# Stick-breaking attention: a PSUM column as the scan's unused operand, and each head's next scores behind its scan

## The reference

```python
z = jnp.einsum('bhqd,bhkd->bhqk', qb, kh).astype(jnp.float32) * (dh ** -0.5)
causal = key_pos[None, :] < q_pos[:, None]
log_keep = jnp.where(causal, -jax.nn.softplus(z), 0.0)
log_after = lax.cumsum(log_keep, axis=3, reverse=True) - log_keep
w = jnp.where(causal, jnp.exp(jax.nn.log_sigmoid(z) + log_after), 0.0)
return jnp.einsum('bhqk,bhkd->bhqd', w.astype(vh.dtype), vh)
```

## Time and profile before

| | us |
|---|---|
| median of 3 runs | 3276.93 (3275.43 to 3278.52) |
| profiled execution | 3275.18 |
| its span in the trace | 3273.3 |
| branch 1 of the stage (first scan to last multiply) | 2241.5 to 2418.2, 176.7 |
| PE / DVE / ACT / POOL busy over the span | 95% / 72% / 39% / 25% |

### The profile page before, as it was taken

The page is one execution under the profiler, slowest core; times in us unless marked ns, Lnnn a source line. Parts: engine busy times, 40 slices in busy tenths (PEclk is TensorE's granted clock), DMA queues, the critical chain, the costliest instruction groups (busy, mean ns, idle before and its releaser), DMA issues.

```text
span 3273.3 us, 37086 instructions
## 1 busy us (share of the span) xinstructions
PE 3122.2 (95%) x14322; PEld 2430.9 (74%) x14322; DVE 2345.3 (72%) x3056; ACT 1285.7 (39%) x2044; POOL 832.0 (25%) x810
## 2 busy tenths in 40 slices
PE   7999998998999999999999999998889989999999
PEld 3577785667787788888877888765467877888787
DVE  6655456886546987778888666587744599989896
ACT  5431114552123433334454333376531344444443
POOL 1212100222111243321001344313643114433101
PEclk9999999999999999999999999999899999999999
DMA  6433461006645222227333345531113422222723
GB/s 229 157 137 118 146 211 52 23 23 227 220 163 174 91 90 84 84 85 282 105 126 117 104 129 180 177 116 41 38 60 117 161 81 87 83 84 75 295 88 109
DMA packets 118296, 406.82 MB, mean 124 GB/s; under 512 B 13704, under 2 KB 16328, under 8 KB 113642
## 3 DMA queue, kind: packets, MB, share of 16 engines
q1 hardware_dynamic: 65626, 200.42, 18.9%
q0 software_dynamic: 52496, 204.04, 17.5%
HBM read 321.50 MB, written 82.90 MB: 124 GB/s over the span
## 4 chain that ended last, share of the span: by engine, by line
PE 64%; DVE 8%; ACT 2%; issue 2%; POOL 1%; DMA 0%; ACTq 0%; DVEq 0%; POOLq 0%
PE PS L455 19%; PE PS L456 19%; PE PS L457 19%; PE PS L3316 2%; PE PS L3355 2%; PE PS L3338 1%; DVE HL L411 1%; POOL Sc L3564 1%; DVE E L3490 1%; ACT HL L393 0%; PE PS L2978 0%; DVE HT L1963 0%; DVE H L3616 0%; DVE HTf L1846 0%; DVE cvr L2182 0%
## 5 line engine op out<-in xcount | busy, mean ns | idle before, releaser
L455 PE MATMUL PS<-H,HL 128*128 128x512 f32 x1920 | 759.9, 396 | 15.9 <-DVE H L3616 7.3
L457 PE MATMUL PS<-H,HL 128*128 128x512 f32 x1920 | 751.3, 391 | 0.0
L456 PE MATMUL PS<-H,HL 128*128 128x512 f32 x1920 | 751.3, 391 | 0.0
L393 ACT ACTIVATE HL<-RAW 128x512 fp32r<-128x512 f32 (+1 forms) x429 | 312.0, 728 | 616.5 <-PE PS L457 560.5
L411 DVE TENSOR_TENSOR HL<-RAW,HL 128x512 fp32r<-128x512 f32 (+1 forms) x429 | 402.3, 938 | 141.7 <-ACT HL L393 132.2
L455 PEld LDWEIGHTS PS<-H,HL 128*128 128x128 f32 x1920 | 362.8, 189 | 105.9 <-issue 19.9
L456 PEld LDWEIGHTS PS<-H,HL 128*128 128x128 f32 x1920 | 362.8, 189 | 76.4 <-issue 2.6
L457 PEld LDWEIGHTS PS<-H,HL 128*128 128x128 f32 x1920 | 362.6, 189 | 76.4
L455 PE MATMUL PS<-HT,HL 128*128 128x512 f32 x720 | 282.7, 393 | 17.9 <-DVE rows L2285 15.8
L456 PE MATMUL PS<-HT,HL 128*128 128x512 f32 x720 | 281.7, 391 | 0.0
L457 PE MATMUL PS<-HT,HL 128*128 128x512 f32 x720 | 281.4, 391 | 0.0
(11 more groups left out here) (457 smaller groups left out, 5700.6 us busy)
## 6 DMA issues: line engine op xcount, KB each, us to landing
RAW<-in_w_up SPq DMA_DIRECT2D x100, 512.0 KB, 3.5
RAW<-in_w_down SPq DMA_DIRECT2D x82, 512.0 KB, 3.8
RAW<-in_w_proj SPq DMA_DIRECT2D x48, 512.0 KB, 3.6
scr_hid<-hidr POOLq DMA_DIRECT2D x36, 512.0 KB, 2.9
RAW<-in_w_wmodr SPq DMA_DIRECT2D x32, 512.0 KB, 4.3
HL<-in_w_dfwd POOLq DMA_DIRECT2D x16, 1024.0 KB, 6.8
HL<-in_w_dinv POOLq DMA_DIRECT2D x16, 1024.0 KB, 5.2
RAW<-in_w_wout SPq DMA_DIRECT2D x26, 512.0 KB, 4.5
```

What stands on the lines that cost most here:

```text
L393: e.activation(part_slot(k, p)[0], src, ACT.Copy).then_inc(*k.high.mark(j, x))
L455: e.matmul(out, lh, rh, start=first, stop=False, skip_group_check=goes_on)
L456: e.matmul(out, lh, rl, start=False, stop=False, skip_group_check=goes_on)
L457: return e.matmul(out, ll, rh, start=False, stop=last, skip_group_check=goes_on)
```

## The change

Three things are changed, all in branch 1:

1. The scan's unused operand becomes the last column of the unit's own scores in PSUM, repeated n times by a stride of zero. So the scan has one operand in SBUF and one in PSUM. For this the scan also waits until take is done, and the last bank of a head's scores is now released by the scan and not by take (the first bank of a wide unit still by take).
2. PE's order in iteration u: turn items 0 and 1, scores of u + 2 for h0, half of the values, turn items 2 and 3, scores of u + 2 for h1. Before, both heads' scores came first and alternated piece by piece.
3. ACT's order: the copy of item 2 of u now comes ahead of keep and take of u + 2 for h1.

```diff
-    def scores(u):
+    def scores(u, heads=(0, 1)):
...
-            for hh in range(2):
+            for hh in heads:
                 b, r = 2 * hh + (at + a) // 512, slice(64 * hh, 64 * hh + 64)
                 claim(b)
...
-                free[b] = [s.dve.at("biased", u, hh) if br == 0 else s.act.at("take", u, hh)]
+                free[b] = [s.dve.at("biased", u, hh) if br == 0 else s.dve.at("left", u, hh) if a + w == n else s.act.at("take", u, hh)]
...
+        later = u + 2 < NU and UNITS[u + 2][0] == 1
+        if u + 2 < NU and not later:
             scores(u + 2)
         if u < NU:
             turn(u, (0, 1))
+        if later:
+            scores(u + 2, (0,))
         if u >= 2:
             values_of((u - 2) // 2, u % 2)
         if u < NU:
             turn(u, (2, 3))
+        if later:
+            scores(u + 2, (1,))
...
+        if u < NU:
+            turn(u, (2, 3))
         if later:
             exponents(u + 2, 1)
-        if u < NU:
-            turn(u, (2, 3))
...
         e.wait_ge(*s.act.at("keep", u, hh))
-        e.tensor_tensor_scan(keep, keep, keep, 1.0, ALU.mult, ALU.bypass).then_inc(*s.dve.mark("left", u, hh))
+
+        e.wait_ge(*s.act.at("take", u, hh))
+        unused = scores_of(k, u, hh)[:, n - 1:n].to_broadcast([128, n])
+        e.tensor_tensor_scan(keep, keep, unused, 1.0, ALU.mult, ALU.bypass).then_inc(*s.dve.mark("left", u, hh))
```

More of the change, by code:

```diff
@@ L3371, in pe_att2 @@
     for u in range(NU + 2):
-        if u + 2 < NU:
+        later = u + 2 < NU and UNITS[u + 2][0] == 1
+        if u + 2 < NU and not later:
             scores(u + 2)
```

## The result

The changed kernel takes 3354.3 us (median of 4 runs, 3352.1 to 3358.9) against 3277.7 for the kernel before on the same chip. The ratio is 1.0236, with a 95% interval from 1.0218 to 1.0254. The forecast was 3288 with a range up to 3303: the sign was right, the loss is 77 us instead of 11. The profiled execution took 3356.5, its span 3354.7.

The account below looks back on a forecast made before the run. Serial scans and multiplies (41 of some 44.7 us a pair) were the first bound, PE's chain close behind. Four pairs of 44.0 + 3 us make 188 against 176.7, +11.3, so median 3288; own range 3280 to 3297, overall 3262 to 3303.

Parts of the forecast that it names:

- Scan and multiply side by side: DVE scans and POOL multiplies: a PSUM operand lets them overlap, opening up to 16 us a pair.
- No longer scan from PSUM: DVE scan: reading one operand from PSUM adds 0; the skill's figures would give an estimated 0.065 us each.
- Single-head scores, +9.4 us a pair: PE's scores: splitting the heads ends their overlap and pays the 9.4 us a pair twice.
- The walk at full clock, 44.0 us a pair: One pair stepped through t = 0 to 7 in the new order with waits, PE at full clock: 44.0 us.
- t = 7: Last iteration of the walked pair, including a 1.9 us wait for the second head's multiply: put at 6.65 us.
- item 2's copy: PE waits for ACT's copy of item 2, behind first-head keep and take: 1.75 us at t = 4, 2.15 at t = 5.
- the release of the last bank by the scan never decides: PE's scores: the first head's scan ends before their second piece is due, nearest at t = 3, 13.4 against 14.2 us.
- The clock, 3 us a pair: PE: about two falls to half clock a pair, partly hidden in waits, cost 3 us, ends 0 and 7.
- rival D: PE's clock decides fully: three falls a pair, all on PE, 51 us a pair, +27, 3304 us; chance 0.12.
- A, the freed lock wins: DVE and POOL's serial 41 us was the true bound; a pair costs 40.3 us, total 3260; chance 0.22.
- C: DVE and POOL: a PSUM-operand scan still excludes the multiply; some 50 us a pair, +21, 3298 us; chance 0.06.
- B: Whole stage: walk right, clock falls cost no more than before, effects cancel; -0.7 us, 3276 us; chance 0.18.

Follow-up runs that it names:

- e4: Changed kernel with branch 1's score matmuls taking all 128 rows, so a head's scores are the sum over both heads (timing only): 3297.8 us, ratio 1.0057.
- e5: e4 plus ACT's value sum moved ahead of item 2's copy and the second head's sigmoids (timing only): 3279.8 us, ratio 0.9989.
- e2: Changed kernel with ACT's value sum moved ahead of item 2's copy and the second head's sigmoids: 3327.0 us, ratio 1.0142.
- e14: e1 with ACT's value sum ahead of the second head's sigmoids: 3337.2 us, ratio 1.0177.
- e9: Kernel before with each head's scores followed directly by its own all-row mask matmul, at the old place with the old scan: 3290.5 us, ratio 1.0035.
- e13: Kernel before with turn items 0 and 1 moved ahead of both heads' scores, ACT's order and scan as before: 3310.0 us, ratio 1.0091.
- e1: Changed kernel with the scan's old SBUF operand and take releasing every bank, so only the new order is left: 3346.1 us, ratio 1.0203.
- e6: Kernel before with all score pieces of head 0 issued before those of head 1, then both masks: 3278.1 us, ratio 0.9997.

## Why the prediction was wrong

**Scan and multiply side by side: right.** Clean durations in every kernel with the operand in all scans: scan of 1024 columns 2.28 us, multiply 2.00. DVE was forecast at 28.5 us a pair and has 26.6 to 27.2, POOL at 23 and has 20.4 to 23.0. The Trainium skill (SBUF — State Buffer, "SBUF: two separate sides") has the lock against GpSimd for a DVE instruction with two inputs in SBUF; the traces agree with it (a multiply of 895 columns takes up to 3.67 us in the kernel before and 1.77 now).

**No longer scan from PSUM: right.** 2283 ns against 2.28 us. The 0.065 us a scan estimated from the Trainium skill (VectorE: DVE Perf Modes, the section on the TRN2 errata) was not seen.

**Single-head scores, +9.4 us a pair: right in kind, and nearly in size at full clock.** e4, at a mean clock of 0.95, has 79.4 us of scores against 53.3 before (53.3 itself holds half clock), 26 more in four pairs where 37.6 were forecast. The doubled sum itself was 75.2 for four pairs, and e5 has 74.2. In after they are 63 more, the rest being the clock.

**The walk at full clock, 44.0 us a pair: its sum was right for the kernel that it described, in part by luck.** (Its terms add up to 43.8: t = 7 gives 6.55 and not 6.65.) e5 has 43.3 a pair. PE's work was forecast at 146.8 us in four pairs and is 145.3. Of the waits, item 2's copy was forecast at 18.2 us and PE waits 13.6 for it; the multiply at 9.6, and it is 6.4; the scan's bank at nothing, and it is 5.3; and 7 us of half clock are in e5 besides. But the kernel of the walk was not the changed one. The walk said that "the release of the last bank by the scan never decides". It gave DVE's value sum its 0.42 us of work and no wait. This is the first step that failed: ACT's value sum comes behind the second head's sigmoids, which the split put last on PE; DVE waits for it in front of the scan of head 0. Its size is 17.9 us (e4 to e5), 4.5 a pair at full clock, and rather more, since e5 still has 23.0 of e4's 50.4 us of DVE's wait. The wait for item 2's copy, which the walk did have, is there in after as well (L3338 for ACT WT L3418: 6.0 us at PE, 9 times, the longest 1.0).

**The clock, 3 us a pair: the second step that failed, and the larger.** The mechanism was named, the size not. I took two falls a pair of 6.8 us each, as in the earlier trace rows. There is one a pair, and it lasts 34 to 55 us: it came behind the pair's longest wait, which is the one the walk missed, and it ended with the value matmuls over all rows. e4 against after puts its price at 56.6 us, 14 a pair; my upper end was 7, and rival D's 27 us in all. The size depends on the order of the steps: with the wait taken off first, it is 27.3 us for the wait (after to e2) and 47.2 for the clock (e2 to e5), for the wait also brings on the fall. What was wrong is the picture of the rise: I let the clock come back by itself after 6.8 us, where rows of the kernel before had shown only falls of 6.8 to 10 us.

**The sum.** By medians 76.6 us = 56.6 (clock, after to e4) + 17.9 (missed wait, e4 to e5) + 2.1 (e5 to before). By the ratios to each set's own before it is 59 + 22 - 4. The last term is the whole walk, doubled scores and new order against the freed lock: the walk put it at -0.7, and the two ways of measuring put it at +2 and -4 (interval of the ratio 0.9979 to 0.9999), so it is near zero and its sign is open.

**The rivals.** A, the freed lock wins, failed: no kernel is clearly faster than before. But the freed lock is not without worth: e5 has 21 us more of scores than before and is level, which the freed lock may have paid for, and e2 is 10 us ahead of e14. (The sums of A and C are also off by 1 to 2 us: 4 x 40.3 gives 3261, 4 x 50 gives 3300.) B's condition, falls that cost no more than before, was met with the change's order only in e4 and e5 (21 and 7 us of half clock), and e5's time is B's. C is excluded by the durations. D had the direction of the truth; its price, three falls of 6.8 us, had the same fault as the forecast's, and was added up too low: three falls cost 3 x 3.4 = 10.2 us a pair, which makes 54.2 and not 51, some 3317 in all and still 37 short.

What stays open: why the half clock lasts. Shown is that it goes when the scores fill all 128 rows (e4), that neither single-head scores (e9) nor the later scores (e13) alone bring more than 72 us of it, and both together 140 (e1). By which measure of the array's work the chip decides, no run here tells.

## What to carry to other kernels

Price a fall of the clock by what PE will run while it is down. Here, with work over half the rows of the array, one matmul at a time, the half clock lasted 34 to 55 us where it had lasted 6.8 to 10 beside both heads' scores; so give such a fall an upper end that reaches to the next long run of matmuls over all rows (here the twelve of the values). When an instruction of one engine is moved behind another's, follow every instruction that stands behind it in its queue (here ACT's value sum) to the engines that wait for it, and count their waits, not their work. And before an edit frees an engine, look in the chain of waits for how much that engine holds: scan and multiply together had 19% of the chain, and the bank that paid for their freedom lay on the engine with 63%.

## What the runs showed of the hardware

- The same instruction stream ran at a granted clock of 0.67 over 64 rows and 0.95 over 128 (after, e4), with PE busy 93% and 79% of the stage. More idle time and the higher clock went together.
- A fallen clock stayed at 0.50 for 54.6 us with PE 95% busy. All four falls in after came behind PE's longest wait of a pair, 1.3 to 1.6 us; all four rises came with twelve value matmuls over 128 rows, near the start of a pair, where the scores are shortest.
- Matmuls in different halves of the rows overlap even when all pieces of the first head stand ahead of those of the second (e6: in a unit of 640 columns, 2340.80, four matmuls of each, eight in 1.36 us); one matmul over all rows between them ends that (e9, scores from 53 to 77 us busy).
- A scan with one operand in PSUM and one in SBUF takes as long as with SBUF alone, 2.28 us for 1024 columns, and runs beside a multiply of GpSimd with neither longer.
